# Three rounded passes for half of the contraction of 19 projection units, with POOL making the low parts

## The reference

```
mod = jax.nn.silu(c) @ mod_w + mod_b
h = rms_norm(x, g_pre_mix) * (1 + scale1) + shift1
(sc_b, sc_c, sc_x, q, k, v, z, xbc, dt_raw, gl_a, gl_b, gl_c) = split_columns(h @ w_in)
merged = sigmoid(gl_a) * y_a + sigmoid(gl_b) * y_b + sigmoid(gl_c) * y_c
```

## Time and profile before

| what | value |
|---|---|
| median of 3 runs | 1276.41 us (1271.58 to 1277.11) |
| the profiled execution | 1271.49 us |
| its span | 1269.8 us |
| granted PE clock, mean | 0.963 |
| busy: PE, DVE, ACT, POOL | 89%, 66%, 36%, 33% |

### The profile page before, as it was taken

How to read it: one execution, slowest core, us unless ns; L and a number is a source line. 1 busy time by engine, 2 the same in 40 slices (tenths; PEclk the granted TensorE clock), 3 DMA queues, 4 the chain that set the end, 5 groups by cost and what they waited for, 6 DMA issues and landing times.

```text
span 1269.8 us, 14565 instructions
## 1 busy us (share of the span) xinstructions
PE 1126.9 (89%) x4566; PEld 733.5 (58%) x4566; DVE 843.4 (66%) x1927; ACT 459.8 (36%) x1090; POOL 417.1 (33%) x351
## 2 busy tenths in 40 slices
PE   4999999998999997999799999887876978788776
PEld 3888888848999995975555655332322323233222
DVE  6554448456888887662988865858668577585454
ACT  2114041034333335342445344343433434334344
POOL 0000000014445551400445445453544434444310
PEclk8999999998999998999899999998999998989999
DMA  9665665563668764452999999999999999999994
GB/s 382 270 230 234 232 246 186 221 233 133 254 286 329 289 277 194 156 234 108 361 402 408 422 421 421 421 421 421 421 422 421 421 421 421 421 421 421 421 421 187
DMA packets 57228, 413.06 MB, mean 325 GB/s; under 512 B 6480, under 2 KB 6480, under 8 KB 7120
## 3 DMA queue, kind: packets, MB, share of 16 engines
q0 software_dynamic: 42912, 311.97, 59.8%
q1 hardware_dynamic: 14112, 100.10, 20.0%
q10 hardware_dynamic: 144, 0.26, 0.1%
HBM read 411.26 MB, written 1.05 MB: 325 GB/s over the span
## 4 chain that ended last, share of the span: by engine, by line
PE 59%; DMA 27%; DVE 7%; ACT 4%; issue 2%; POOL 0%; SPq 0%; DVEq 0%; ACTq 0%; POOLq 0%
PE ps L979 15%; PE ps L450 14%; DMA gate_area<-in_experts,idx 8%; DMA areaB<-in_experts,idx 8%; DMA ring<-in_experts,idx 6%; PE ps L463 6%; PE ps L465 6%; PE ps L464 5%; DMA small<-in_experts,idx 3%; PE ps L695 2%; PE ps L547 2%; PE ps L890 2%; DMA areaB<-in_mod_w 2%; PE ps L430 1%; PE ps L531 1%
## 5 line engine op out<-in xcount | busy, mean ns | idle before, releaser
L1284 ACT ACTIVATE act<-now 128x1 f32<-128x1 f32 x256 | 50.9, 199 | 262.2 <-DVE now L2028 259.8
L979 PE MATMUL ps<-areaB,mod_sum 128*128 128x512 f32 x248 | 122.8, 626 | 23.3 <-ACT mod_sum L1291 23.3
L450 PE MATMUL ps<-hT,ring 128*128 128x256 f32 x608 | 134.0, 380 | 0.0
L450 PEld LDWEIGHTS ps<-hT,ring 128*128 128x128 f32 x608 | 114.7, 190 | 15.5 <-issue 0.2
L463 PE MATMUL ps<-hT_h,w_lo 128*128 128x256 f32 x416 | 118.6, 285 | 5.0 <-POOL hT_l L1368 3.9
L1361 POOL TENSOR_TENSOR w_lo<-ring,w_hi 128x512 fp32r<-128x512 f32 x41 | 101.0, 2478 | 63.3 <-ACT w_hi L1074 63.1
L1520 DVE SCALAR_TENSOR_TENSOR mod_sum<-mod_ring,cols,mod_sum 128x256 f32<-128x256 f32 x294 | 119.2, 482 | 0.0
L465 PE MATMUL ps<-hT_h,w_hi 128*128 128x256 f32 x416 | 118.6, 285 | 0.0
L464 PE MATMUL ps<-hT_l,w_hi 128*128 128x256 f32 x416 | 117.4, 282 | 0.0
L979 PE MATMUL ps<-ring,mod_sum 128*128 128x512 f32 x204 | 99.8, 623 | 15.1 <-ACT mod_sum L1291 15.1
L1410 POOL DMA_INDIRECT areaB<-in_experts,idx x62 | 69.4, 1120 | 130.6 <-DVE idx L1965 61.5
(11 more groups left out here) (366 smaller groups left out, 2144.9 us busy)
## 6 DMA issues: line engine op xcount, KB each, us to landing
ring<-in_stream SPq DMA_DIRECT2D x75, 1024.0 KB, 5.9
mod_ring<-in_mod_w POOLq DMA_DIRECT2D x40, 1024.0 KB, 6.9
gate_area<-in_mod_w SPq DMA_DIRECT2D x3, 1024.0 KB, 13.2
areaB<-in_mod_w SPq DMA_DIRECT2D x3, 1024.0 KB, 23.1
gate_area<-in_stream SPq DMA_DIRECT2D x3, 1024.0 KB, 11.7
mod_ring<-in_mod_w SPq DMA_DIRECT2D x2, 1024.0 KB, 5.9
mod_ring<-in_stream SPq DMA_DIRECT2D x2, 1024.0 KB, 10.4
small<-in_small SPq DMA_DIRECT2D x1, 1352.0 KB, 28.8
```

The lines of the kernel that those rows point to most:

```text
L450: last = mm(ps[:, bank, b * T:(b + 1) * T], w[:, at:at + P], rhs[:, k, :], start=(k == 0), stop=(k == KC - 1))
L979: last = mm(ps[:, B3 + 2 * t + b, :], spread_w[n // FEW % 2][:, n % FEW, :], row[ROW_OF[n]][:, D + 512 * b:D + 512 * b + 512], start=first ...
```

## The change

The units from sc 1 to gl 11 (`FRONT0` = 4 to `FRONT1` = 23, 19 units) keep the first four chunks of the contraction as fp32 products; the other four are made in three rounded passes. The order inside a unit changes to: the first half for both blocks, a wait for the low part, the second half for both blocks. ACT rounds the second half of `hT` and of each unit's weights, behind the copy of unit u-2 for unit u. POOL subtracts. The rounded parts have two buffers each, in `spare` and `xn`; those of `hT` lie in `mT`.

Modulation units 8 to 23 are issued by SP, in pairs, behind the loads of weight units 2, 7, 10, 13, 15, 16, 18 and 20, each with the wait on `mod_summed` that POOL had. POOL issues 24 to 29, behind its last subtraction. Their semaphores and those of the eight query loads are shared differently.

```diff
+FRONT0, FRONT1 = AT["sc", 1], AT["gl", 11] + 1
+MOD_SP = 24
+MODS_BEHIND_LOAD = {2: 8, AT["sc", 1] + RING: 10, AT["qk", 1] + RING: 12, AT["z", 1] + RING: 14,
+                    AT["gl", 1] + RING: 16, AT["gl", 2] + RING: 18, AT["gl", 4] + RING: 20, AT["gl", 6] + RING: 22}
...
+        def second_half(u):
+
+            if u == AT["v", 0]:
+                return cut(slot[u % RING], UNIT // 2, 2, UNIT // 4)
+            return slot[u % RING].rearrange("p (b h n) -> p b h n", b=2, h=2)[:, :, 1, :]
...
+        front_hi = [rounded(f"front_hi{n}", "spare", n * UNIT // 2, 2, UNIT // 4) for n in range(2)]
+        front_lo = [rounded(f"front_lo{n}", "xn", n * UNIT // 2, 2, UNIT // 4) for n in range(2)]
+        hq_h, hq_l = rounded("hq_h", "mT", 0, 4, T), rounded("hq_l", "mT", 4 * T, 4, T)
...
@@ SP
-            with sp.Fori(1, edge) as i:
+            def front_mods(u):
+
+                if u in MODS_BEHIND_LOAD:
+                    for m in (MODS_BEHIND_LOAD[u], MODS_BEHIND_LOAD[u] + 1):
+                        sp.wait_ge(mod_summed, m - 1)
+                        sp.dma_start(mod_place(m), mod_w[m]).then_inc(mod_arrived(m)[0], 16)
+
+            front_mods(RING - 1)
+            for i in range(1, edge):
                 for s in range(RING):
                     load(i, s, False)
+                    front_mods(RING * i + s)
...
@@ PE
             def proj_T(kind, j):
-                w = arrived(kind, j)
-                gemm_T(w, bank_free(), hT).then_inc(unit_done, 1)
+
+                u, w, bank = AT[kind, j], arrived(kind, j), bank_free()
+                if u < FRONT0:
+                    gemm_T(w, bank, hT).then_inc(unit_done, 1)
+                    return
+                for b in range(2):
+                    for k in range(4):
+                        at = (b * KC + k) * P
+                        mm(ps[:, bank, b * T:(b + 1) * T], w[:, at:at + P], hT[:, k, :], start=(b == 0 and k == 0),
+                           stop=False, skip_group_check=True)
+                both = front_parts(u)
+                for b in range(2):
+                    for k in range(4):
+                        last = mm3(ps[:, bank, b * T:(b + 1) * T], [v[:, b, k * P:(k + 1) * P] for v in both],
+                                   [v[:, k, :] for v in (hq_h, hq_l)], False, k == 3, skip_group_check=True)
+                last.then_inc(unit_done, 1)
...
@@ ACT
+            def split_front(u):
+
+                act.wait_ge(w_in[u % RING], 16 * (u // RING + 1))
+                act.wait_ge(unit_done, u - 1)
+                A(front_hi[u % 2], second_half(u), ACT.Identity).then_inc(front_hi_ready, 1)
...
+            act.wait_ge(hT_act, KC)
+            A(hq_h, hT[:, 4:KC, :], ACT.Identity).then_inc(hq_hi_ready, 1)
+            split_front(FRONT0)
             for j in range(3):
                 copy_out("sc", j, sc[:, 2 * j:2 * j + 2, :], bank=n % 2)
+                split_front(n + 2)
                 n += 1
...
@@ POOL
-            load_mods(MOD_EARLY, MOD_FRONT + 2)
+            def split_front(u):
+
+                pool.wait_ge(front_hi_ready, u - FRONT0 + 1)
+                nc.gpsimd.tensor_tensor(front_lo[u % 2], second_half(u), front_hi[u % 2].bitcast(F32),
+                                        ALU.subtract).then_inc(front_lo_ready, 1)
+
+            pool.wait_ge(hq_hi_ready, 1)
+            nc.gpsimd.tensor_tensor(hq_l, hT[:, 4:KC, :], hq_h.bitcast(F32), ALU.subtract).then_inc(hq_lo_ready, 1)
+            for u in range(FRONT0, FRONT1):
+                split_front(u)
+            load_mods(MOD_SP, MOD_FRONT + 2)
```

More of the change, by code:

```diff
@@ L203, in mod_arrived, with query_arrived @@
                 return mod_early_in[m], 16
-            return mod_in[m % 2], 16 * ((m - MOD_EARLY) // 2 + 1)
+            if m < MOD_SP:
+                return mod_early_in[m % 2], 16 * ((m - MOD_EARLY) // 2 + 2)
+            return mod_in[m % 2], 16 * ((m - MOD_SP) // 2 + 1)
+        def query_arrived(h):
+            return mod_early_in[h], 32 if h >= 2 else 16 * ((MOD_SP - MOD_EARLY) // 2 + 2)
         xbc_raw = cut(areaA, 0, 6, T + 3)
@@ L270, in build @@
         w_in = [sem(f"w_in{s}") for s in range(RING)]
-        query_in = {h: sem(f"query_in{h}") for h in range(HEADS)}
         wo2_in = sem("wo2_in")
@@ L486, in bank_free, with front_parts @@
                 return n % 2
-            def proj_T(kind, j):
-                w = arrived(kind, j)
-                gemm_T(w, bank_free(), hT).then_inc(unit_done, 1)
+            def front_parts(u):
+                if u == FRONT0:
+                    pe.wait_ge(hq_lo_ready, 1)
+                pe.wait_ge(front_lo_ready, u - FRONT0 + 1)
+                return front_hi[u % 2], front_lo[u % 2]
+            def proj_T(kind, j):
+                u, w, bank = AT[kind, j], arrived(kind, j), bank_free()
[13 more added lines that the diff above has]
+                last.then_inc(unit_done, 1)
             def transposes(n):
@@ L579, in _ @@
             for t in range(NT):
-                for k in range(KC):
-                    last = mm(ps[:, bank, t * T:(t + 1) * T], hT[:, k, t * P:(t + 1) * P], w[:, k * T:(k + 1) * T],
-                              start=(k == 0), stop=(k == KC - 1))
+                for k in range(4):
+                    mm(ps[:, bank, t * T:(t + 1) * T], hT[:, k, t * P:(t + 1) * P], w[:, k * T:(k + 1) * T],
+                       start=(t == 0 and k == 0), stop=False, skip_group_check=True)
+            both = front_parts(AT["v", 0])
+            for t in range(NT):
+                for k in range(4):
+                    last = mm3(ps[:, bank, t * T:(t + 1) * T], [v[:, k, t * P:(t + 1) * P] for v in (hq_h, hq_l)],
+                               [v[:, k // 2, (k % 2) * T:(k % 2 + 1) * T] for v in both], False, k == 3,
+                               skip_group_check=True)
             last.then_inc(unit_done, 1)
@@ L1125, in _ @@
                 copy_out("gl", j, gates[:, 2 * j:2 * j + 2, :], func=ACT.Sigmoid, bank=n % 2)
+                if n + 2 < FRONT1:
+                    split_front(n + 2)
                 n += 1
```

7 lines of the change are left out of this document (5 added, 2 removed).

## The result

The changed kernel takes **1262.55 us** (median of 4 runs, 1261.20 to 1265.11), the kernel before 1275.49 beside it (4 runs, 1271.58 to 1277.11): ratio 0.9902, interval 0.9886 to 0.9918. The two profiled executions took 1261.20 and 1271.49 us, 10.3 apart. The change is faster by 1%.

What follows compares the result with a forecast made beforehand. TensorE was taken to bound the kernel until 265 us; passes save 11.3 us, waits on VectorE's line leave 3.9, 2 are given back: 2 us less, 1274.5. The range is 1265 to 1286, the forecast's own 1270 to 1281.

Steps and rivals of the forecast that it cites:

- What bounds the kernel: From 60.92 to 265.30 us the chain is TensorE alone, so a microsecond saved there moves all that follows.
- Step 1: TensorE's projection units: three rounded passes for half a unit take 6.31 us instead of 6.91; 19 units save 11.3 us.
- Steps 2, 3 and 6: ScalarE's roundings about 1.04 us each, POOL's subtractions 2.4, both covered; modulation pair 24 issued at about 205, costing 0.
- Step 4: POOL's subtraction holds a VectorE instruction with two SBUF inputs, such as modulation products: some 2.1 us per collision.
- rival B: Slower: POOL pieces of 2.9 us lengthen VectorE's pairs, SP holds weight loads, ScalarE's roundings wait; 9 us slower, 1285; chance 0.18.
- step 3: POOL's subtractions: 2.4 us each; copy to hand-overs 4.3 us after unit u-2, wanted 9.8 after, so covered.
- Step 5: Modulation loads moved to SP's queue: a pair lands 7.3 us after issue (7.0 to 8.5); late weight loads cost nothing.
- The sum along VectorE's line: Collisions end pair 20 at 178.7; TensorE waits 5.3 us for decay arguments, 2.6 for squares; 3.9 of 11.3 us remain.
- The clock: A TensorE wait of 5 us could bring its lower 1.2 GHz level; nothing up to 2.6 us of slower work.
- A: Rival: collisions on VectorE are rare, pair 20 done at 173.2, gain kept; 8 to 11 us less, 1266; chance 0.27.
- C: Rival: rounded passes beside fp32 products in one accumulation start 0.144 us apart and bring nothing; 1276; chance 0.05.

Runs made afterwards that it cites:

- E3: Changed kernel with each of POOL's subtractions of weights made twice, one behind the other; 1304.46 us, ratio 1.0225.
- E7: Changed kernel with VectorE's modulation products waiting at three new places for the instruction just before, which puts gaps into the stream; 1280.4 us, ratio 1.0041.
- E8: E7's gaps in the changed kernel, with POOL subtracting only 8 of 512 columns from the projections on; 1268.15 us, ratio 0.9947.
- E4: Changed kernel with the loads of modulation units 8 to 23 left on POOL's queue, between its subtractions, instead of SP's; 1269.61 us, ratio 0.9961.
- E6: Changed kernel with six of eight chunks in rounded passes instead of four, for units sc 1 to gl 6; 1277.54 us, ratio 1.0015.
- E9: Changed kernel with the four branch units also half in rounded passes (8 of their 16 products); 1262.75 us, ratio 0.9901.
- E10: Changed kernel with branch and output units also in rounded passes, eight units more; 1259.07 us, ratio 0.9878.
- E5: Separate kernel without the reference: 72 bursts of 22 VectorE instructions, one POOL subtraction in each, three kinds of burst; POOL pieces timed, no kernel time.
- E1: Kernel before with only the loads of modulation units 8 to 23 moved to SP, no passes, roundings or subtractions; 1274.31 us, ratio 0.9994.

## Why the prediction was wrong, point by point

**What bounds the kernel**: right. TensorE had the chain up to 254.65, and what was saved there arrived: the landing behind it began 10.65 us earlier (265.30 against 254.65). It took 5.77 us instead of 5.19, so 10.1 reached the rounding.

**Step 1, TensorE**: right. 0.59 us a unit where 0.60 was forecast, 19 x 0.59 = 11.2, of which 10.65 came through. Three rounded passes for half a unit cost 24 x 0.119 = 2.86. By the ratio of four passes to three, which the Trainium skill (FP8 and Floating Point Precision, "TensorE Precision Notes") gives for true fp32, the pitch would be 3.46 + 2.59 = 6.05 us; the trace has 6.32, so four to three doesn't hold as a ratio of times.

**Steps 2, 3 and 6**: right. A rounding took 1.05 us in the mean (forecast 1.04), a POOL piece 2.35 to 2.6 us unless it waited (forecast 2.4), and pair 24 went out at 199.69 (forecast 205) and started at 207.76 (forecast 214) without anybody waiting for it.

**Step 4, what POOL takes from VectorE, is the step that failed.** Its price was right, 2.1 us, in the changed kernel (pair 12) as in E3 and E7. Its count was near (from pair 12 on, E7 has exactly the pieces per pair that the forecast listed). Wrong was the sentence "while POOL reads two tensors, a VectorE instruction with two SBUF inputs stands still", read as the only outcome. It was drawn from one collision of the feed-forward part, which POOL happened to win. The same rows had the other outcome: POOL's 41 pieces there took 2.80 us in the median and 1.29 alone. The forecast saw it, under rival B, and set it aside as a wait for one long instruction, where here each lasts 0.4 us. But in a modulation pair a piece mostly waited for the end of the whole stream, at its own cost, and POOL could afford it: it had 9.8 - 4.3 = 5.5 us of slack by step 3, and the longest piece took 3.7 more than 2.4.

In the changed kernel pairs 8 to 22 met eight pieces: two held VectorE, both in pair 12, and six waited (a ninth began 0.35 us ahead of the end of pair 12). In E7 none waited, and the time rose by 12.3 us over E8. Added to the changed kernel's 1262.55 that gives 1274.9, close to the forecast of 1274.5; the closeness is partly luck, since the forecast had 7.9 us of waits and no price for the clock, and E7 has 6.2 and 5.0.

Shown: the outcome decides the time, and with the gaps POOL goes first each time. Not shown: what decides it without gaps, at pair 12 and in the first convolution, where POOL went first three times of three. It isn't chance from one execution to the next: a piece that came 1.11 us into pair 12 went first in all six traces that have it (changed kernel, E3, E4, E6, E9, E10).

The Trainium skill (SBUF — State Buffer, "SBUF: two separate sides") calls the pair of ports that the two engines share an exclusive lock, which whoever starts first keeps for the whole instruction. The trace agrees for POOL's side (VectorE stands for the whole of one piece, 2.56 us in E5) and goes further for VectorE's: 14 of 24 pieces in E5 waited not for the one instruction under way but for the 15 or 16 that started after it, 0.40 us apart.

**Step 5, the loads**: right as a sum of its own (E1: 0.7 us, within the interval), and its landing was within its bounds: pairs 16 and 18 began 6.98 and 7.05 us behind the end of the pair before (7.3 forecast, 7.0 at least), pairs 14 and 20 8.47 and 8.41 (8.5 at most). What it didn't see is that the price depends on the passes: with the loads left on POOL the same change gives 7 us less (E4).

**The sum along VectorE's line** fell with step 4: pair 20 done at 171.1 instead of 178.7, waits of 0.2 instead of 7.9. Its logic held: E4 has the wait at the decay arguments, and E7's delays from pair 12 to 22 are the forecast's. Two slips in it are small: pairs 18 and 20 start 6.9 and 7.1 us behind the pair before and not 7.3, and the last step adds up to 202.7, not 202.9.

**The clock** wasn't put to the test in the changed kernel: TensorE hardly waited, and its granted clock was 1.00 from 75 to 260 us. Where it waited, the clock fell, and that cost 1.7 us behind a wait of 2.6 (E4) and 5.0 behind waits of 2.9 and 3.3 (E7); the forecast allowed for it and put nothing into its sum.

**The rivals**: A's mechanism, the gain kept because VectorE isn't held, is what happened, though not for the reason it gave. The pieces do fall into the pairs; most of them wait there. B is the mechanism of E3 and E6, and of one wait of E7, where POOL's pieces had their forecast length: the forecast's own world held 2.9 us of it; in the changed kernel its condition isn't met (pair 20 was to be done after 182). C is excluded by the pitch.

**The size**: A's 1266 was 3.5 above the measured median. Both profiled executions lie below their medians, the one of before by 4.0, the one of after by 1.35; between the profiled ones it is 10.3.

## What to carry to other kernels

When a helper engine gets work beside VectorE, ask of each collision not only what it costs but who will wait, and give the wait to the engine with slack. In the modulation pairs here a stream of VectorE instructions without gaps and a buffer ahead of the consumer did so for six pieces of eight, while three waits put into the stream gave every collision to POOL. It is no guarantee: in the first convolution, a stream of the same pitch, POOL went first each time, and so did each piece directly behind one that had gone first. So look for the outcome in the trace. A share of busy time can't tell it; the durations of one engine's pieces can (a group with a median of 2.5 us and a maximum of 6.1 is waiting). A move that does nothing by itself can be what makes another pay, so test it with the other part in place as well as alone.

## What the runs showed of the hardware that was not expected

- POOL against VectorE with two SBUF inputs: a piece of 1024 elements took either 2.35 to 2.63 us or 8.59 to 8.94, to the end of the burst (E5). With a wait on the instruction before, POOL went first in 24 of 24; with a PSUM input neither waited (2.35 us, VectorE 0.477 each).
- A VectorE TENSOR_SCALAR with one input in SBUF can be held too: 2.33 us instead of 0.17 at 75.54 in the changed kernel, 2.52 instead of 0.62 for the two ahead of pair 18 in E4.
- The same modulation loads landed in 5.8 us (SP, changed kernel), 7.0 (SP, E1), 6.8 (POOL, before) and 7.2 (POOL, E4); where they took 5.8, the weight loads took 6.5 instead of 4.8 or 4.9.
- The start of an execution varies: the granted clock between 30 and 45 us was 0.95 in one execution and 0.80 in another, in kernels that don't differ there, and with the stretch behind it that came to 3.75 us. From 58 to 75 us it was 1.00 in the traces of the kernel before, the changed kernel and E10, and 0.90 in the eight others of this kernel. Differences of 2 us need the trace beside the time.
